# Selected and banded attention of a prompt: probabilities and values in two parts, masks by matrix product, sums kept by tile

## The reference, cut to what matters

```python
def slc_attend(q, sel, idx, valid, pos):       # selected blocks
    mask = jnp.repeat(valid, SLC_BLOCK, axis=-1) & (kpos <= pos[None, :, None, None])
    s = jnp.einsum('bqghd,bqgkd->bqghk', q, k) * (HD ** -0.5)
    p = masked_softmax(s, mask[:, :, :, None, :])
    return jnp.einsum('bqghk,bqgkd->bqghd', p, v)
def win_prompt(q_rot, kv_win):                 # a window of 512 keys
    mask = (d >= 0) & (d <= WINDOW) & (kpos[:, None, :] >= 0)
    ...
def nsa_merge(gates, o_cmp, o_slc, o_win):
    return (gates[..., None] * jnp.stack([o_cmp, o_slc, o_win], axis=2)).sum(2)
```

## Time and profile before

| | |
|---|---|
| median of 3 runs | 2675.48 us (2673.27 to 2676.08) |
| the profiled execution | 2675.98 us |
| its span, first to last instruction | 2674.1 us |
| mean granted TensorE clock | 0.950 of 2.4 GHz |
| busy over the span | PE 91%, DVE 45%, ACT 30%, POOL 12% |
| the stage of the change | 841 to 1154 us |

### The profile page before, as it was taken

One profiled execution on the slowest core, in us unless ns is written; L12 is line 12 of the kernel. 1 busy time (PEld: TensorE's weight loads), 2 busy tenths in 40 slices (PEclk: granted clock), 3 DMA queues, 4 the chain that ended last, 5 costly groups with the idle time before them and its releaser, 6 DMA issues. The chain is left out here.

```text
span 2674.1 us, 40420 instructions
## 1 busy us (share of the span) xinstructions
PE 2442.7 (91%) x15394; PEld 2195.9 (82%) x15394; DVE 1216.5 (45%) x2151; ACT 812.1 (30%) x1783; POOL 322.0 (12%) x567
## 2 busy tenths in 40 slices
PE   6976788899877899979979999999999999999999
PEld 6966588899766688954459999997899999999997
DVE  4446466412636766645551223234433333333334
ACT  5254155345334555512231212121321111111110
POOL 1003321003101422245400000000000000000000
PEclk9989599899998999979889999999999999999999
DMA  4010432421110000046611111212121111111111
GB/s 151 17 32 15 132 104 91 111 107 40 42 34 1 1 1 1 2 122 170 156 46 36 48 48 48 79 50 85 48 64 46 37 45 48 48 48 48 48 32 64
DMA packets 216620, 156.77 MB, mean 59 GB/s; under 512 B 76706, under 2 KB 197589, under 8 KB 216372
## 3 DMA queue, kind: packets, MB, share of 16 engines
q1 hardware_dynamic: 191204, 124.15, 16.1%
q0 software_dynamic: 8096, 18.98, 2.6%
q10 hardware_dynamic: 17136, 11.12, 1.4%
HBM read 142.76 MB, written 15.59 MB: 59 GB/s over the span
## 5 line engine op out<-in xcount | busy, mean ns | idle before, releaser
L177 PE MATMUL ps<-brT_r,ff_wih 128*128 128x344 f32 x1008 | 322.0, 319 | 0.0
L179 PE MATMUL ps<-brT_r,ff_wi_r 128*128 128x344 f32 x1008 | 321.6, 319 | 0.0
L178 PE MATMUL ps<-xnT_r,ff_wih 128*128 128x344 f32 x1008 | 321.3, 319 | 0.0
L3668 ACT ACTIVATE ff_sa<-ps 128x344 f32<-128x344 f32 x66 | 30.2, 458 | 563.4 <-PE ps L179 563.3
L177 PE MATMUL ps<-x_r,mg_wh 128*128 128x344 f32 x576 | 184.9, 321 | 6.9 <-DVE xnT_r L165 6.9
L177 PEld LDWEIGHTS ps<-brT_r,ff_wih 128*128 128x128 f32 x1008 | 189.6, 188 | 1.0
L179 PEld LDWEIGHTS ps<-brT_r,ff_wi_r 128*128 128x128 f32 x1008 | 189.4, 188 | 0.0
L178 PEld LDWEIGHTS ps<-xnT_r,ff_wih 128*128 128x128 f32 x1008 | 189.0, 187 | 0.4
L178 PE MATMUL ps<-xnT_r,mg_wh 128*128 128x344 f32 x576 | 184.3, 320 | 0.0
L3704 DVE TENSOR_TENSOR x<-x,ps 128x512 f32<-128x512 f32 (+1 forms) x198 | 134.9, 686 | 100.9 <-PE ps L179 100.2
L179 PE MATMUL ps<-x_r,mg_w_r 128*128 128x344 f32 x552 | 176.2, 319 | 0.0
(11 more groups left out here) (605 smaller groups left out, 5863.1 us busy)
## 6 DMA issues: line engine op xcount, KB each, us to landing
ff_wi<-in_w_ffn_in SPq DMA_DIRECT2D x42, 512.0 KB, 5.0
mg_w<-in_w_in SPq DMA_DIRECT2D x23, 512.0 KB, 3.9
ff_wo<-in_w_ffn_out SPq DMA_DIRECT2D x11, 1024.0 KB, 4.9
s_pages<-in_cache_kv_slc POOLq DMA_DIRECT2D x128, 64.0 KB, 2.8
s_pages<-in_cache_kv_slc SPq DMA_DIRECT2D x128, 64.0 KB, 2.8
sc_X<-in_cache_kv_cmp SPq DMA_DIRECT2D x56, 128.0 KB
sc_X<-in_cache_kv_cmp POOLq DMA_DIRECT2D x56, 128.0 KB, 2.4
mg_w<-in_w_branch SPq DMA_DIRECT2D x23, 256.0 KB, 4.3
```

The lines of the kernel that those rows point to most:

```text
L177: nc.tensor.matmul(out, wh, xh, start=(first and k == 0), stop=False)
L178: nc.tensor.matmul(out, wh, xl, start=False, stop=False)
L179: ins = nc.tensor.matmul(out, wl, xh, start=False, stop=(last and k == n - 1))
L3668: nc.scalar.activation(sa[:, s % 2, :], ps[:, s % 2, 0:BLK], ACT.Silu).then_inc(silued, 1)
```

## The change

Four things change, and some memory moves.

1. Values are split once, in `stage_turn`: `high` on ScalarE and `low` on VectorE, twice each, and they lie side by side in the place of key and value (the keys have been transposed by then).
2. Every item of probabilities gets a high part `pTh` from ScalarE and then a low part `pTl` from VectorE; `by_act` is gone. A value product becomes two, in reduced fp32, which stream high and low values side by side. `item_low` releases an item's bank.
3. The masks are cast once to reduced fp32 by ScalarE, and TensorE adds them into the scores by a product with the identity. VectorE's L2003 and L2004 are gone.
4. Results are summed for a tile and head in `sums` over both branches, 128 columns wide (against high values, against low values), and two additions at a tile's end bring them into the accumulator.

```diff
@@ stage_turn
+                for t in range(0, QT, 4):
+                    ins = high(nc, v_hi[:, t:t + 4], v_raw[:, t:t + 4])
+                ins.then_inc(vhigh, 1)
                 act.wait_ge(hid, 1)
...
+                dve.wait_ge(vhigh, 1)
+                for t in range(0, QT, 4):
+                    ins = low(nc, v_lo[:, t:t + 4], v_raw[:, t:t + 4], v_hi[:, t:t + 4])
+                ins.then_inc(vlow, 1)
+                dve.wait_ge(vlow, 1)
@@ stage_slc_win
-            if done_a[m]:
-                eng.wait_ge(pkept_a, done_a[m])
-            if m - done_a[m]:
-                eng.wait_ge(pkept_v, m - done_a[m])
+            if m:
+                eng.wait_ge(item_low, m)
...
+        def item_up(act, m, u):
+            bank, hi, twin, _ = parts(m, u)
+            act.wait_ge(pturned, m + 1)
...
+            if u >= 2:
+                act.wait_ge(attended, u - 1)
+            high(nc, hi, bank).then_inc(item_high, 1)
+
+        def item_down(dve, m, u):
+            bank, hi, twin, lo = parts(m, u)
+            dve.wait_ge(item_high, m + 1)
...
+            low(nc, lo, bank, hi).then_inc(item_low, 1)
...
                         nc.tensor.matmul(out, qA[:, i % 2, h, :], kk, start=True, stop=False)
+                        if u == 0:
+                            pe.wait_ge(masks_ready, 3)
+                        if a == 0 and br == 1 and i >= 4:
+                            nc.tensor.matmul(out[:, 0:P], one[:, :], band[:, :], start=False, stop=False)
+                        if a + n == hi - lo:
+                            nc.tensor.matmul(out[:, (n - 1) * P:n * P], one[:, :], causal[:, :], start=False, stop=False)
                         ins = nc.tensor.matmul(out, qB[:, i % 2, h, :], kk, start=False, stop=True)
...
-                        kv = kvsw[:, lo + b, br * 256 + g * 128:br * 256 + (g + 1) * 128]
-                        ins = nc.tensor.matmul(ps[:, 6 + u % 2, 0:P], pT[:, u % 2, b * P:(b + 1) * P],
-                                               kv, start=(b == 0), stop=(b == hi - lo - 1))
+                        kv = A["kvswR"][:, lo + b, br * 256 + g * 128:br * 256 + (g + 1) * 128]
+                        for x in (pTh, pTl):
+                            ins = nc.tensor.matmul(ps[:, 6 + u % 2, 0:P], x[:, u % 2, b * P:(b + 1) * P], kv,
+                                                   start=(b == 0 and x is pTh), stop=(b == hi - lo - 1 and x is pTl))
...
-                    pe.wait_ge(used, (i + 1) * 2 * H)
+                    pe.wait_ge(summed, i + 1)
...
-                    if br == 1 and i >= 4:
-                        chain.link(dve, nc.vector.tensor_tensor(s[:, 0:P], s[:, 0:P], c("band"), ALU.subtract))
-                    chain.link(dve, nc.vector.tensor_tensor(s[:, n - P:n], s[:, n - P:n], c("causal"),
-                                                            ALU.subtract))
...
+                    if br == 0:
...
+                        nc.vector.tensor_scalar(o, ps[:, 6 + u % 2, 0:P], f[:, k:k + 1], None, ALU.mult).then_inc(used, 1)
+                        return
...
+                    if h == H - 1:
+                        dve.wait_ge(used, u + 1)
...
+                        chain.link(dve, nc.vector.tensor_tensor(dst, dst, by_part[:, :, :, 0, :], ALU.add))
+                        nc.vector.tensor_tensor(dst, dst, by_part[:, :, :, 1, :], ALU.add).then_inc(summed, 1)
```

More of the change, by code:

```diff
@@ L1810, in stage_slc_win @@
     first_item.append(len(items))
[L1812 to L1816, removed]
     NU = len(units)
@@ L1824, in stage_slc_win @@
         p_ = st.sb("p", [P, 2, S])
[L1825 to L1828, removed]
+        pTh = st.sb("pTh", [P, 2, S], FR)
+        pTl = st.sb("pTl", [P, 2, S], FR)
+        sums = st.sb("sums", [P, H, P])
+        one, causal, band = (qflat[:, x:x + P] for x in (32 * P, 33 * P, 34 * P))
+        small = A["q"][:, :, :].rearrange("p t n -> p (t n)")
+        mx, sm, f = (small[:, x:x + 4] for x in (35 * P, 35 * P + 4, 35 * P + 8))
@@ L1829, in stage_slc_win @@
+        minus = small[:, 35 * P + 12:35 * P + 13]
         sem = st.sem
         shared, pchain = sem("shared"), Chain(sem("share_step"))
[L1831 to L1833 removed]
+        zeroed, scored, maxed, exped, pturned, item_high, item_low, attended, used, oturned, okept = (
+            sem(n) for n in ("zeroed", "scored", "maxed", "exped", "pturned", "item_high", "item_low",
@@ L1847, in keep @@
             if kind == "q":
[L1848 to L1860, removed]
@@ L1861, in keep @@
-                return
-            if by_act[m] != (eng is nc.scalar):
-                return
[L1864 to L1871, removed]
+                at = lambda x, rows: x[rows, a % 2, HPG * n:HPG * (n + 1), :].rearrange("p h q -> p (h q)")
@@ new lines, in parts @@
+                return ps[0:HD, 4 + m % 2, :], at(qA, slice(0, HD)), at(qA, slice(HD, P)), at(qB, slice(0, HD))
+            cols = slice(a * P, (a + n) * P)
+            return ps[:, 4 + m % 2, 0:n * P], pTh[:, u % 2, cols], None, pTl[:, u % 2, cols]
+        def item_up(act, m, u):
+            bank, hi, twin, _ = parts(m, u)
+            act.wait_ge(pturned, m + 1)
+            if twin is not None:
+                nc.scalar.activation(twin, bank, ACT.Copy, scale=-(HD ** -0.5))
+                nc.scalar.activation(hi, bank, ACT.Copy, scale=-(HD ** -0.5)).then_inc(item_high, 1)
+                return
+            if u >= 2:
+                act.wait_ge(attended, u - 1)
+            high(nc, hi, bank).then_inc(item_high, 1)
@@ new lines, in item_down @@
+        def item_down(dve, m, u):
+            bank, hi, twin, lo = parts(m, u)
+            dve.wait_ge(item_high, m + 1)
+            if twin is not None:
+                if items[m][1] < 2:
+                    dve.wait_ge(zeroed, 1)
+                nc.vector.scalar_tensor_tensor(lo, bank, -(HD ** -0.5), hi.bitcast(F32), ALU.mult,
+                                               ALU.subtract).then_inc(item_low, 1)
+                return
+            low(nc, lo, bank, hi).then_inc(item_low, 1)
@@ L1969, in out @@
                                          ps[:, 7, :].rearrange("p (a q) -> p a q", a=4), ACT.Copy).then_inc(okept, 1)
+                for dst, name, scale in ((one, "ident", 1.0), (causal, "causal", -1.0), (band, "band", -1.0)):
+                    nc.scalar.activation(dst[:, :], c(name), ACT.Copy, scale=scale).then_inc(masks_ready, 1)
                 for m in range(2):
-                    keep(nc.scalar, m, 0)
+                    item_up(act, m, 0)
                 for u in range(NU):
```

25 lines of the change are left out of this document (15 added, 10 removed).

## The result

The changed kernel takes 2706.22 us (median of 4 runs, 2702.08 to 2710.2) against 2674.38. The ratio is 1.0115, 95% interval [1.0103, 1.0127]: slower, by 32 us. The forecast was 2705.5.

What follows compares the result with a forecast made beforehand. ScalarE's turn and the score circuit were taken to bound early tiles, TensorE itself later ones. Terms 9.0 + 7.1 + 5.5 + 6.3 + 1.8 + 1.7 = 31.4 us, taken as 30, gave 2705.5 us; range 2682 to 2732.

Steps and rivals of the forecast that it cites:

- Price of small products: TensorE's value products: 0.112 us per reduced product as per plain record, 1056 before and after, so nothing gained or lost.
- Part 1: Tiles 0 to 3: every unit now goes round ScalarE's turn, where every second did; 9.0 us slower, ends 0 and 15.
- 0.58 + 0.55 + 0.72: ScalarE's turn in tile 2: transposes to copy, copy to exponential, exponential to next transposes; 1.85 us a unit.
- Part 2: Tiles 4 to 7: mask products on TensorE cost 10.6 us, removed VectorE masks give back 3.5; net +7.1.
- Part 3: Next tile's queries wait for VectorE's low part in tiles 4 to 6, 4.5 us; copy order in tiles 0 to 3, 1.0.
- Part 4: Tile boundary: two VectorE additions make the next maximum 0.9 late, 6.3 us; output copy behind a second high part, 1.8.
- Part 5: Both ends of the stage: bare last additions +1.45, three mask casts before the first queries +0.25; together 1.7 us.
- Part 6: Stage before: splitting values on ScalarE and VectorE fits into their idle time; cost 0, without that cover 5 us.
- tile 0's low clock: Tile 0, at its low clock: a guessed +0.15 us a unit for ScalarE's turn.
- C: Rival: in every unit, transposes wait for the low part two items before; 64 units, 20 us more, 2727; chance 0.13.

Runs made afterwards that it cites:

- masks_only: The kernel before with only the mask products and casts of the change, so TensorE adds the masks; ratio 1.0004 [0.9996, 1.0013] to before.
- wide: The changed kernel with value products streaming 256 columns instead of 128, only the own group's result being read; 6.9 us faster than the changed kernel.
- out_first: The changed kernel with ScalarE's output copy of a finished tile ahead of unit 2's probability copies instead of behind them; 20.6 us faster than the changed kernel.
- masks_vector: The changed kernel with masks subtracted by VectorE again, mask products and casts gone; median 8.5 us above the changed kernel's, intervals overlapping.
- vhigh: The changed kernel with VectorE making the odd units' high parts in tiles 0 to 3; median 2706.6 us, single runs 2692.8 to 2712.3.
- b_narrow: The kernel before with value products streaming only the 64 value columns instead of 128; 6.4 us slower than before, ratio 1.0019 [1.0010, 1.0028].

## Why the prediction was right, and where it was not

- Price of small products (0.112 us, no gain from reduced fp32): right, to the third digit.
- Part 1, ScalarE's turn in tiles 0 to 3, 9.0 us: right mechanism, mis-sized. Regular units went from 1.30 to 1.37, 1.62 to 1.69 and 1.97 to 2.01, and tile 0 did not move: 13 x 0.18 = 2.4 us. The step that was off is "0.58 + 0.55 + 0.72": the 0.55 held a wait for VectorE's maximum, which the change shortened.
- Part 2, masks on TensorE, +7.1: measured 4.5, in the changed kernel (pairs +0, +0.11, +0.24, +0.21, 8 a tile) and in masks_only.
- Part 3, the queries' bank, 4.5 + 1.0: two units together have 2.3 us more than regular ones where they had 1.4, six times 0.86 = 5.1 us. Nothing in tiles 0 to 3.
- Part 4, the boundary, 8.1: in `wide`, where the clock is even, units 1 to 4 carry 0.4 to 0.9 more than before, some 4.4 us over 7 boundaries. The additions alone make one exponential 0.9 late, as said (3.35 us from unit 1 to 2 in tile 4 where 2.44 is regular), but this overlaps with the wait behind the output copy, which was there before and grew by 1.3 us (1.8 were forecast).
- Part 5, the two ends, 1.7: the end grew by 1.95, of which some 0.5 is clock (9.1 us in out_first, where the clock is full there, against 7.6). The casts cost nothing: from the first query transposes to the first exponential it is 5.2 us in both. So 1.5.
- Part 6, cost 0: right.

That is 2.4 + 4.5 + 5.1 + 4.4 + 1.5 = 17.9 us in place of 31.4. As a check, wide less its slower products is 319.1 - 5.0 - 301.3 = 12.8 in the tiles and 1.7 at the end, with a tile 0 that is 1.3 us luckier in clock: 16. The clock makes the rest, 12 by the medians and 14 to 16 by these two sums. The prediction took the clock of before for given, and named tile 0's low clock only to guess 0.15. It priced the products by their step alone, and the step is the same whether the columns fill it or half of it (L2107, L2925). So the mechanisms of its parts are there, but that the number came out is luck: an unpriced loss of some 12 and an excess of 13.5 in the terms cancelled. Of the rivals, C did not show: 0.5 us of waits on low parts before ordinary transposes.

What stays open: why the clock falls behind one wait of 1.3 us and not behind the next, and why it fell more often in masks_vector and vhigh than in the changed kernel.

## What to carry to other kernels

Here one plain product of 128 columns became two reduced ones in the same 0.224 us. The step said that this is free, but it halves what the array is fed in that time, and with TensorE waiting between such products the clock went to half, which took some 12 us. When a change makes TensorE's stream thinner, look at the granted clock by stretch first. Do not put a small copy that TensorE needs behind large ones that it doesn't: moving it was worth 6.5 us in the kernel before and 20 in the changed one, 8 of them clock. A step between two rows can hold a short wait that isn't marked; before a step is taken as a price, check when the other input was done.

## What the runs showed of the hardware that was not expected

- Less work can be slower: half the streamed columns in b_narrow cost 6.4 us, twice the columns in `wide` gained 6.9.
- With weights of 128 columns the step is 0.112 us for 64 streamed columns in plain fp32 (b_narrow) and for 128 in reduced fp32 (after) alike, while 256 in reduced fp32 step by 0.119 (`wide`).
- Single executions of one kernel follow the clock: in vhigh 2692.8 and 2693.6 us at 0.945, and 2705.9 to 2712.3 at 0.938 to 0.940.
- Every fall of the clock from tile 2 on came within 2.2 us of the end of a TensorE wait of 1.2 to 1.6 us, and only where reduced products of 128 columns were streamed.
